# Two-layer hybrid encoder: norm chains in halves of the tokens, the last mixing ahead of two squares, a statistic in its own bank, layer 0's first row maximum ahead of six taps

## The reference, cut to what matters

```python
for l in range(2):
    mod = silu(c) @ w_ada[l] + b_ada[l]              # six vectors of 1024: sh1, sc1, g1, sh2, sc2, g2
    h = rms_norm(x, norm1_g[l]) * (1 + sc1) + sh1
    za, zb, zq, zk, zv = split(h @ w_in[l])
    ya = silu(rms_norm(conv31(za_value * sigmoid(za_gate))))   # depthwise, 31 taps, 256 channels
    yb = rms_norm(bg * conv3(cg * hv))                         # depthwise, 3 taps, 256 channels
    # 4 heads, two softmaxes each: (p0 - lam * p1) @ v, then rms_norm per head
    yc = diff_attention(rope(rms_norm(q)), rope(rms_norm(k)), v)
    x = x + g1 * (concat(ya, yb, yc) @ w_out[l])
    h = rms_norm(x, norm2_g[l]) * (1 + sc2) + sh2
    g, u = split(h @ w_gate_up[l])                   # 2 x 2816
    x = x + g2 * ((silu(g) * u) @ w_down[l])
```

## Time and profile before

| | us |
|---|---|
| median of 3 runs (lowest, highest) | 1208.53 (1208.11, 1209.99) |
| the profiled execution | 1210.46 |
| its span | 1208.7 |
| TensorE busy | 1179.4 (98%) |
| VectorE busy | 706.0 (58%) |
| ScalarE busy | 492.6 (41%) |
| GpSimd busy | 117.5 (10%) |
| mean granted TensorE clock | 0.993 |

### The profile page before, as it was taken

One profiled execution on the slowest core, in us unless ns is written; L12 is line 12 of the kernel. 1 busy time (PEld: TensorE's weight loads), 2 busy tenths in 40 slices (PEclk: granted clock), 3 DMA queues, 4 the chain that ended last, 5 costly groups with the idle time before them and its releaser, 6 DMA issues.

```text
span 1208.7 us, 14274 instructions
## 1 busy us (share of the span) xinstructions
PE 1179.4 (98%) x5130; PEld 930.0 (77%) x5130; DVE 706.0 (58%) x1015; ACT 492.6 (41%) x730; POOL 117.5 (10%) x195
## 2 busy tenths in 40 slices
PE   8999999989999999999989999998999999999998
PEld 6787555868888888888868876666888888888887
DVE  7989898976555433566666988755533333333221
ACT  5554787452323232322242558864423223232220
POOL 2411232211112000111000112100000000000000
PEclk9999999989999999999999999999999999999999
DMA  8787346876555323677413664314232322223332
GB/s 304 239 241 174 70 99 193 303 214 220 200 187 185 102 89 104 265 252 247 140 57 117 152 144 101 74 43 132 70 105 87 104 89 102 94 97 105 105 104 87
DMA packets 48939, 175.17 MB, mean 145 GB/s; under 512 B 5697, under 2 KB 5825, under 8 KB 48898
## 3 DMA queue, kind: packets, MB, share of 16 engines
q1 hardware_dynamic: 30386, 107.13, 27.0%
q0 software_dynamic: 18512, 67.51, 19.9%
HBM read 172.52 MB, written 2.10 MB: 144 GB/s over the span
## 4 chain that ended last, share of the span: by engine, by line
PE 81%; DVE 12%; ACT 4%; issue 2%; DMA 2%; DVEq 0%; ACTq 0%; SPq 0%
PE ps L1406 22%; PE ps L1408 21%; PE ps L1407 21%; PE ps L1436 2%; PE ps L1469 2%; PE ps L1467 2%; PE ps L1468 2%; DMA raw<-w_stream 2%; DVE uc L1008 2%; PE ps L1639 1%; DVE w_lo L891 1%; PE ps L1614 1%; PE ps L1440 1%; DVE ada_ring_mid_a L944 1%; DVE ada_ring_first L944 1%
## 5 line engine op out<-in xcount | busy, mean ns | idle before, releaser
L590 ACT ACTIVATE w_hi<-raw 128x1024 fp32r<-128x1024 f32 x196 | 207.8, 1060 | 562.2 <-PE ps L1408 486.5
L891 DVE TENSOR_TENSOR w_lo<-raw,w_hi 128x1024 fp32r<-128x1024 f32 x164 | 201.5, 1229 | 264.8 <-ACT w_hi L590 264.6
L1406 PE MATMUL ps<-h_hi,w_hi 128*128 128x512 f32 x848 | 335.7, 396 | 0.0
L1408 PE MATMUL ps<-h_lo,w_hi 128*128 128x512 f32 x848 | 330.8, 390 | 0.0
L1407 PE MATMUL ps<-h_hi,w_lo 128*128 128x512 f32 x848 | 330.7, 390 | 0.0
L1406 PEld LDWEIGHTS ps<-h_hi,w_hi 128*128 128x128 f32 x848 | 159.4, 188 | 47.7 <-issue 16.3
L1408 PEld LDWEIGHTS ps<-h_lo,w_hi 128*128 128x128 f32 x848 | 159.5, 188 | 33.7
L1407 PEld LDWEIGHTS ps<-h_hi,w_lo 128*128 128x128 f32 x848 | 159.6, 188 | 32.1 <-issue 0.5
L1406 PE MATMUL ps<-gu_hi,w_hi 128*128 128x512 f32 x352 | 136.9, 389 | 0.0
L1407 PE MATMUL ps<-gu_hi,w_lo 128*128 128x512 f32 x352 | 136.9, 389 | 0.0
L1408 PE MATMUL ps<-gu_lo,w_hi 128*128 128x512 f32 x352 | 136.9, 389 | 0.0
(11 more groups left out here) (183 smaller groups left out, 1337.3 us busy)
## 6 DMA issues: line engine op xcount, KB each, us to landing
raw<-w_stream SPq DMA_DIRECT2D x196, 512.0 KB, 3.3
w_lo<-w_stream POOLq DMA_DIRECT2D x32, 512.0 KB, 8.0
ada_ring_gu<-ada POOLq DMA_DIRECT2D x28, 512.0 KB, 4.2
ada_ring_late<-ada POOLq DMA_DIRECT2D x28, 512.0 KB, 4.9
ada_ring_first<-ada POOLq DMA_DIRECT2D x16, 512.0 KB, 5.6
ada_ring_mid_a<-ada POOLq DMA_DIRECT2D x12, 512.0 KB, 6.4
ada_ring_mid_b<-ada POOLq DMA_DIRECT2D x12, 512.0 KB, 5.4
xT<-x_t SPq DMA_DIRECT2D x4, 512.0 KB, 5.6
```

The lines of the kernel that those rows point to most:

```text
L590: act.activation(w_hi[:, u % RING, :], raw[:, u % RAW, :], ACT.Copy).then_inc(s_whi, 1)
L891: dve.tensor_tensor(w_lo[:, u % RING, :], raw[:, u % RAW, :], w_hi[:, u % RING, :].bitcast(F32), ALU.subtract).then_inc(s_wlo, 1)
L1406: pe.matmul(dst, whi, rhs[0][:, n, :], start=start, stop=False)
L1408: return pe.matmul(dst, whi, rhs[1][:, n, :], start=False, stop=stop)
```

## The change

1. `HALVES` splits the 512 tokens in two. At the three norms the last addition to x, its square, its sum, Ln, Exp, the scaling and `h_hi` of chunk 0 are done in halves of 256 tokens with a semaphore each. The sums of the halves go to banks 7 and 4. `h_hi` of both halves is signalled once, behind the second.
2. ScalarE's `step` that stood between the last square and Ln stands in the loop over `h_hi`, at chunk 2; VectorE's `split_lo` of the same unit stands behind the norm, or in it at chunk 3.
3. In layer 0, modulation slices 37 and 38 are done beside the last `w_out` units, and one is left behind the last addition (`M_LATE` from 37 to 38).
4. Layer 0: the six taps ahead of the first row maximum go; three stand behind it, one more in each of the tiles 3, 7 and 12. `QUARTERS`: one quarter goes from tile 2 to tile 0, in both layers.
5. The squares of the short convolution stand behind the mixing of tile 15. Statistic 4 goes to bank 3 and waits for the last Exp of the attention instead of for Ln of statistic 3.

```diff
-M_LATE = M_GU - 3
+M_LATE = M_GU - 2
-TAPS_UNIT = ({6: 4, 9: 4, 10: 6, 13: 2, 14: 7, 15: 6}, {3: 4, 4: 6, 5: 6, 6: 6, 9: 4, 10: 6, 13: 3})
+TAPS_UNIT = ({6: 4, 9: 4, 10: 6, 13: 2, 14: 7}, {3: 4, 4: 6, 5: 6, 6: 6, 9: 4, 10: 6, 13: 3})
+TAPS_FIRST = (3, 0)
-TAPS_TILE = ((3, 3, 3, 2, 1, 3, 3, 3, 3, 2, 1, 3, 1, 0, 0, 0), (2, ...))
-QUARTERS = (0, 2, 2, 1, 2, 1, 2, 1, 2, 1, 2, 1, 1, 1, 1, 0)
+TAPS_TILE = ((3, 3, 3, 3, 1, 3, 3, 4, 3, 2, 1, 3, 2, 0, 0, 0), (2, ...))
+QUARTERS = (1, 2, 1, 1, 2, 1, 2, 1, 2, 1, 2, 1, 1, 1, 1, 0)
-CONV_SQUARE_AT, SHORT_SQUARE_AT = 12, 14
+CONV_SQUARE_AT, SHORT_SQUARE_AT = 12, 15
+HALVES = (slice(0, T // 2), slice(T // 2, T))
+        B_HALF_STAT = (7, 4)
+        B_MIX = (7, 7, 7, 7, 3, 7)
# ScalarE
+            def square_halves(n):
+                act.wait_ge(s_sum, (KC - 1) * (n - 1) + KC - 2)
+                act.wait_ge(s_xhalf, n)
+                a, b = HALVES
+                act.activation(wa[:, 1, a], xT[:, KC - 1, a], ACT.Square).then_inc(s_sqhalf, 1)
+                act.wait_ge(s_xnew, KC * n)
+                act.activation(wa[:, 1, b], xT[:, KC - 1, b], ACT.Square).then_inc(s_sq, 1)
+            def rstd_halves(n):
+                for half, c in enumerate(HALVES):
+                    stat, ln, rs = (s_nstat, s_nln, s_nrs) if half else (s_sthalf, s_lnhalf, s_rshalf)
+                    act.wait_ge(stat, n + half)
+                    act.activation(rstd[:, 0, c], ps[:, B_HALF_STAT[half], c], ACT.Ln, ...).then_inc(ln, 1)
+                    act.wait_ge(ln, n + half)
+                    act.activation(rstd[:, 0, c], rstd[:, 0, c], ACT.Exp, scale=-0.5).then_inc(rs, 1)
+            def hi_halves(l, which):
+                ...
+                act.wait_ge(s_thalf, n)
+                act.activation(h_hi[:, 0, first], wb[:, 0, first], ACT.Identity, bias=mod[:, l, a:a + 1])
+                act.wait_ge(s_t, KC * n + 1)
+                act.activation(h_hi[:, 0, second], wb[:, 0, second], ...).then_inc(s_hhi, 1)
-                step(U + U_OUT + N_OUT - 1)
-                norm_rstd(2 * l + 1)
+                square_halves(2 * l + 1)
+                rstd_halves(2 * l + 1)
                 act.wait_ge(s_gain, 2 * l + 1)
-                for k in range(KC):
+                hi_halves(l, 1)
+                for k in range(1, KC):
+                    if k == 2:
+                        step(U + U_OUT + N_OUT - 1)
# VectorE
+            def apply_halves(l, which):
+                for half, c in enumerate(HALVES):
+                    ...
+                    dve.scalar_tensor_tensor(wb[:, 0, c], xT[:, 0, c], gain[...], rstd[:, 0, c], ...)
+            def add_halves(l, bank, g, unit):
+                dve.wait_ge(s_unit, unit)
+                ...
+                for c, done in zip(HALVES, (s_xhalf, s_xnew)):
+                    dve.scalar_tensor_tensor(xT[:, n, c], ps[:, bank, c], mod[...], xT[:, n, c], ...).then_inc(done, 1)
                 row_max(l, 0)
+                conv_a_taps(l, TAPS_FIRST[l])
                 row_inverse(l, 0)
-                    for m in range(M_LATE, M_GU):
-                        mod_dot(m)
+                    mod_dot(M_GU - 1)
                 norm(l, 1)
+                split_lo(U + U_GU + RING - 1)
# TensorE
             def norm_stat(n):
-                pe.matmul(ps[:, B_STAT, :], ones[:], sq_sum[:], start=True, stop=False)
-                pe.wait_ge(s_sq, KC * (n + 1))
-                pe.matmul(ps[:, B_STAT, :], ones[:], wa[:, 1, :], start=False, stop=True).then_inc(s_nstat, 1)
+                for b, c in zip(B_HALF_STAT, HALVES):
+                    pe.matmul(ps[:, b, c], ones[:], sq_sum[:, c], start=True, stop=False)
+                for b, c, squared, count, done in zip(B_HALF_STAT, HALVES, (s_sqhalf, s_sq), (n, KC * (n + 1)),
+                                                      (s_sthalf, s_nstat)):
+                    pe.wait_ge(squared, count)
+                    pe.matmul(ps[:, b, c], ones[:], wa[:, 1, c], start=False, stop=True).then_inc(done, 1)
             def mix_stat(l, k):
-                if k:
+                if B_MIX[k] != B_STAT:
+                    pe.wait_ge(s_exp, 2 * N_TILES * (l + 1))
+                elif k:
                     pe.wait_ge(s_mln, 6 * l + k)
```

More of the change, by code:

```diff
@@ L874, in _ @@
                     for j in range(3):
-                        if not last and 3 * n + j == N_DOWN - 1:
-                            square_x(2 * l + 2, n)
-                        step(U + U_DOWN + 3 * n + j, split=not last or 3 * n + j < N_DOWN - RING)
+                        if last or 3 * n + j < N_DOWN - 1:
+                            step(U + U_DOWN + 3 * n + j, split=not last or 3 * n + j < N_DOWN - RING)
                     if not last and n < KC - 1:
@@ L880, in _ @@
                 if not last:
-                    norm_rstd(2 * l + 2)
+                    square_halves(2 * l + 2)
+                    rstd_halves(2 * l + 2)
         @block.vector
@@ L976, in norm_lo, with norm @@
                                          h_hi[:, k, :].bitcast(F32), ALU.add, ALU.subtract).then_inc(s_h, 1)
-            def norm(l, which):
-                dve.wait_ge(s_nrs, 2 * l + which + 1)
+            def apply_halves(l, which):
+                n = 2 * l + which
+                for half, c in enumerate(HALVES):
+                    if half:
+                        dve.wait_ge(s_nrs, n + 1)
+                    else:
+                        dve.wait_ge(s_rshalf, n)
+                    dve.scalar_tensor_tensor(wb[:, 0, c], xT[:, 0, c], gain[:, l, which, 0:1], rstd[:, 0, c], ALU.mult,
+                                             ALU.mult).then_inc(s_t if half else s_thalf, 1)
+            def norm(l, which, u=None):
                 dve.wait_ge(s_gain, 2 * l + which)
                 for k in range(KC + 1):
-                    if k < KC:
+                    if k == 0:
+                        apply_halves(l, which)
+                    elif k < KC:
                         norm_apply(l, which, k)
@@ L986, in norm @@
                         norm_lo(l, which, k - 1)
+                    if k == 3 and u is not None:
+                        split_lo(u)
             def conv_input(l):
@@ L1208, in _ @@
                 else:
-                    norm(l, 0)
+                    norm(l, 0, U + RING - 1)
                     first = 0
@@ L1326, in _ @@
                         make_gain(0, 1)
+                    if s == N_OUT - 1:
+                        add_halves(l, B_OUT[s], G1, U + U_OUT + s + 1)
+                        break
                     add_to_x(l, s, B_OUT[s], G1, U + U_OUT + s + 1)
                     split_lo(U + U_OUT + s + RING)
-                    beside = list(range(M_MID + 12, M_LATE))[2 * s:2 * s + 2] if l == 0 else []
+                    beside = []
+                    if l == 0 and s < N_OUT - 1:
+                        m = M_MID + 12 + 2 * s - max(s - 4, 0)
+                        beside = list(range(m, m + (2 if s < 4 else 1)))
                     for m in beside[:1]:
@@ L1377, in _ @@
                         u = U + U_DOWN + 3 * n + j
-                        if j == 2:
+                        if j == 2 and n == KC - 1 and not last:
+                            add_halves(l, B_DOWN + n % 2, G2, u + 1)
+                        elif j == 2:
                             add_to_x(l, n, B_DOWN + n % 2, G2, u + 1)
-                        if not last or 3 * n + j < N_DOWN - RING:
+                        if 3 * n + j < N_DOWN - (RING if last else 1):
                             split_lo(u + RING)
@@ L1497, in mix_stat @@
                 for i, z in enumerate(zs):
-                    mm = pe.matmul(ps[:, B_STAT, :], ones[:], mix_sq(z), start=i == 0, stop=i == len(zs) - 1)
+                    mm = pe.matmul(ps[:, B_MIX[k], :], ones[:], mix_sq(z), start=i == 0, stop=i == len(zs) - 1)
                 mm.then_inc(s_mstat, 1)
```

28 lines of the change are left out of this document (24 added, 4 removed).

## The result

The changed kernel takes 1200.18 us (median of 6 runs, 1196.81 to 1200.52) against 1209.00 for the kernel before beside it on the same chip (6 runs, 1207.91 to 1210.68): the medians differ by 8.8 us. The ratio of the two sets of runs, which is not the quotient of the medians (0.9927), is 0.9916, 95% interval 0.9905 to 0.9927, which is 10.2 us (8.8 to 11.5). 10.5 were forecast, 1198.0 for the median. The profiled execution took 1200.52 with a span of 1198.4, so 2.12 lie outside the span where 1210.46 - 1208.7 = 1.76 lay before.

The account below looks back on a forecast made before the run. TensorE was busy almost throughout, so only its idle time and the half clock behind it could be won. Norms 2.9 + 1.3 + 0.9 + 0.9, maximum 2.0, attention ends 1.0 + 1.5 gave 10.5 us: median 1198.0, range 1192.5 to 1203.5.

Parts of the forecast that it names:

- Halves, 0.9 each: At each of the three norms, the chain in halves of 256 columns shortens from 5.72 to 4.8 us.
- Its upper bound for the cost: Norm chain if halves cost as much as wholes: 0.36 + 6.6 + 0.3 = 7.1, a loss of 1.3 us.
- Rival A: Halves pay too little and VectorE keeps the attention's gain: 6.3 us gained, 1202.2; chance 0.18.
- Layer 0's second norm, 2.9 and 1.3: Stretch from last addition falls from 7.73 to 4.8 us (2.9); the chunks behind it from 13.9 to 12.6 (1.3).
- One of its signs of being wrong: In the first gate-up units, TensorE waiting for a weight's low part would show the prediction wrong.
- Lost clock elsewhere, 0 with 1.5 to either side: At the other two norms idle shrinks only from 3.1 to about 2.6, so lost clock stands: 0, -1.5 to +1.5 each.
- Rival B: Shorter idle time keeps the clock at 2.4 GHz behind the norms: 14.1 us gained, 1194.4; chance 0.15.
- First row maximum, 2.0: Layer 0's attention: moving the taps removes TensorE's waits and lost clock (3.7), VectorE keeps 2.0 us (0.5 to 3.7).
- Ends of the attentions, 1.0 and 1.5: Mixing ahead of the squares and the statistic in bank 3 gain 1.0 us in layer 0, 1.5 in layer 1.
- The new wait costs nothing: End of layer 1's attention: squares end at 789.3, just when TensorE is free, so waiting for them costs nothing.
- The sum, 10.5 against 8.8: Norms 2.9 + 1.3 + 0.9 + 0.9, maximum 2.0, ends of attention 1.0 + 1.5: 10.5 us gained, median 1198.0.
- Rivals C and D: C: moved work does not matter, 1206.0, chance 0.05. D: layer 0's tile loop repeatedly loses clock, 1211.6, chance 0.04.

Follow-up runs that it names:

- the clock held: Kernels timed with unread products behind the norms' statistics on TensorE: kernel before 1203.76, halves undone 1198.62, steps set back 1198.85, end as before 1198.35; changed kernel 1195.85.
- the loads moved: Changed kernel with GpSimd's four loads of modulation weights put behind the low parts of gate-up units 3 and 4: 1200.22, ratio 0.9919 to the kernel before.
- idle products: 128x128 products nobody reads, put behind the three norms' statistics; in the changed kernel (12, 10, 10): 1195.85, ratio 0.9887; in the kernel before (22, 13, 13): 1203.76.
- the second profile: Profile of the changed kernel run once more, unaltered: 1200.52 (1196.96 to 1201.01).
- whole slices: Changed kernel with the norm chains' last slice whole again (halves undone): 1203.57, ratio 0.9947 to the kernel before; with unread products behind the statistics 1198.62.

## Why the prediction was right

- **Halves, 0.9 each.** Right: 1.04 and 1.00. Addition 0.48, square 0.42, Ln 0.47, Exp 0.42, scaling 0.48 and h_hi 0.51 came out within 0.01 of the estimates; the first half's sum is read 0.73 behind its start (829.35 to 830.08), where 0.69 stood without its hand-over. What the reasoning did not have is that the halves need the moved steps: alone they give 0.25 and 0.62. The prediction put the step only on layer 0's path and drew the new path at the others as if it were free of it. Its upper bound for the cost is added up wrongly (0.36 + 6.6 + 0.3 is 7.3, not 7.1), which no forecast rests on, and the 0.42 that it calls the trace's was then worked out from rows at 32 and 512 columns; measured it is 0.42. Rival A falls. In this chain so does the advice of the Trainium skill (VectorE: DVE Perf Modes, the section on the TRN2 errata) to take tiles of at least 512 elements, which was on that rival's side; its fixed cost is real (0.42 for half of 0.63).
- **Layer 0's second norm, 2.9 and 1.3.** Right in size, 2.54 and 1.41, though in part by luck. One of its signs of being wrong came true, a wait for a low part: 3.04, about 0.5 beyond h_hi. With the clock held, chain and chunks together gave 1.78 (from the norm's sum, 18.46 before and 16.68 after) and not 3.95. So more than half of this gain was a raw unit that happened to land late in the profile, and clock. The chunks at full clock took 11.00 before and 11.82 after, where I had 11.0 and about 12.0; so the 1.3 was clock regained and no work saved, and it was not there in every execution: with the loads moved, the clock over 245 to 261 was 0.79 and the chunks took 13.84.
- **Lost clock elsewhere, 0 with 1.5 to either side.** Right as bounds: -1.21 behind layer 1's second norm and nothing between the layers. Rival B came about in two of twelve executions only (1196.81 and 1196.96); in the others 2.54 still loses the clock. Its number, 1194.4, was nearly reached when the idling was filled.
- **First row maximum, 2.0.** Right: 1.87, and TensorE keeps what VectorE keeps. Both waits went, the clock rose from 0.98 to 1.00, and VectorE's new wait of 0.69 stands in tile 5. In its run with idle products, which stand only behind the norms, the kernel before happened to have 1.00 there too (70 us from 120), and its loop is no shorter: 70.79 from the first scores to tile 13, against 70.47. The 1.4 of lost clock was not on the path.
- **Ends of the attentions, 1.0 and 1.5.** Right: 1.11 and 1.66, in the second profile 1.12 and 1.39, and 2.5 for both by the comparison with the clock held. "The new wait costs nothing" was wrong by 0.35 in either layer: TensorE came sooner than I had it, and waits for the squares.
- **The sum, 10.5 against 8.8.** What it missed: 0.36 outside the span, 1.2 of clock at the end, 0.4 in layer 0's norm; the profile hides part of this by 0.88 before the attention, in unchanged code. By the ratio the gain is 10.2, so the sum was not shown to be too large; but 1 to 3 us of it are clock and landing, as told above. Rivals C and D fell with the parts.

The best version here is the change with the idle products: 1195.85, 13.7 under the kernel before beside it.

## What to carry to other kernels

A serial chain through several engines gains by halves although each instruction pays its fixed cost twice, provided that nothing else stands in the narrow engine's queue between them; look at what was hidden there before. Where a stretch's clock falls after an idle time, as here after 2.5 us, fill that time before tuning anything by 1 or 2 us: it brought 4.7 here and made the comparisons sharp. A gain read off one profile that holds a landing or a slow stretch is worth only its part that returns in a second one.

## What the runs showed of the hardware

- The time outside the span depends on the kernel: 1.72 to 1.83 in every run of the kernel before and of both kernels with whole slices, 2.07 to 2.19 in every run of those with halves. These use six semaphores more and have 14316 instructions instead of 14274. The number of instructions as a whole is not it: the kernel before with idle products has 14466 and stays at 1.74 to 1.80, the changed kernel with them has 14444 and 2.08 to 2.16. Whether it is the semaphores, or the instructions more on ScalarE (742 for 730) and VectorE (1021 for 1015), wasn't tried.
- TensorE idle for 2.54 us was enough for its clock to fall to 1.2 GHz behind it, in each of the three norms of the second profile of the changed kernel (0.89 over 245 to 261, 0.96 over 600 to 640, 0.94 over 830 to 860); but not each time, as two of twelve executions had a mean of 0.999. The gap of 0.31 that was left behind the idle products did not do it (1.00).
- Between executions of the same code the slow stretch behind one norm was worth 1.2 us more or less, and a 512 KB unit landed up to 1.9 us late or in time.
